# Router shift on VectorE, expert-stage ends by halves, the norm's scale on a diagonal, fillers at the last load

## What is computed

```
h  = rms_norm(x, norm1_g) * (1 + scale1) + shift1
x  = x + gate1 * mixer(h)
h  = rms_norm(x, norm2_g) * (1 + scale2) + shift2
x  = x + gate2 * hier_moe(h)
```

## Time and profile before

| | |
|---|---|
| median of 3 runs | 1050.4 us (1048.04 to 1050.93) |
| the profiled execution's own time | 1042.98 us |
| span of its trace | 1041.2 us |
| mean granted TensorE clock | 0.949 of full speed |
| PE busy | 905.2 us, 87% of the span |
| DVE, ACT, POOL busy | 314.3, 197.3, 34.2 us |
| moved by DMA | 329.18 MB, mean 316 GB/s |
| chain that ended last | PE 70%, DMA 19%, DVE 3%, SP's queue 3%, ACT 2% |

### The profile page before, as it was taken

How to read it: one execution, slowest core, us unless ns; L and a number is a source line. 1 busy time by engine, 2 the same in 40 slices (tenths; PEclk the granted TensorE clock), 3 DMA queues, 4 the chain that set the end, 5 groups by cost and what they waited for, 6 DMA issues and landing times.

```text
span 1041.2 us, 14206 instructions
## 1 busy us (share of the span) xinstructions
PE 905.2 (87%) x5967; PEld 516.2 (50%) x5967; DVE 314.3 (30%) x774; ACT 197.3 (19%) x366; POOL 34.2 (3%) x62
## 2 busy tenths in 40 slices
PE   1799999979699787997699999999996997789963
PEld 0586556664565444564244444444445654455531
DVE  1120235831732111110277814231037221111203
ACT  3111112340211100100340013543002111111102
POOL 3000000111000000000000000001000000000000
PEclk9899999999799999998889999999997998899987
DMA  9999746999597999999943555146835979999995
GB/s 313 401 389 373 284 172 235 409 414 401 191 408 275 421 421 420 421 421 416 394 174 127 191 193 217 41 162 255 348 137 211 377 299 420 422 420 419 421 416 218
DMA packets 74088, 329.18 MB, mean 316 GB/s; under 512 B 5773, under 2 KB 6149, under 8 KB 50213
## 3 DMA queue, kind: packets, MB, share of 16 engines
q1 hardware_dynamic: 69012, 313.44, 76.0%
q0 software_dynamic: 4400, 13.35, 3.5%
q10 hardware_dynamic: 608, 1.44, 0.4%
HBM read 322.11 MB, written 6.09 MB: 315 GB/s over the span
## 4 chain that ended last, share of the span: by engine, by line
PE 70%; DMA 19%; DVE 3%; SPq 3%; ACT 2%; issue 1%; DVEq 0%
PE PS L763 68%; DMA ring<-in_moe_w_gate 11%; DMA ring<-in_mod_w 5%; DMA ring<-in_moe_w_down 4%; SPq L635 1%; SPq L642 1%; SPq L648 1%; ACT scratch L1421 0%; ACT HT L1428 0%; DVE H L1819 0%; DVE X L1814 0%; PE PS L796 0%; DVE scratch L2013 0%; PE PS L1363 0%; PE PS L1093 0%
## 5 line engine op out<-in xcount | busy, mean ns | idle before, releaser
L763 PE MATMUL PS<-ring,scratch 128*32 128x256 f32 (+3 forms) x2592 | 294.5, 461 | 58.8 <-DMA ring<-in_moe_w_gate 39.7
L763 PEld LDWEIGHTS PS<-ring,scratch 128*32 128x32 f32 (+2 forms) x2592 | 140.2, 127 | 205.8 <-issue 158.1
L763 PE MATMUL PS<-ring,HT 128*128 128x512 f32 x432 | 191.9, 598 | 2.7 <-ACT HT L1428 1.9
L763 PEld LDWEIGHTS PS<-ring,HT 128*128 128x128 f32 x432 | 81.2, 191 | 99.2 <-issue 95.5
L763 PE MATMUL PS<-scratch 128*128 128x512 f32 (+3 forms) x480 | 115.9, 427 | 4.6 <-DVE scratch L2477 2.9
L763 PE MATMUL PS<-scratch,H 128*128 128x128 f32 x640 | 84.2, 288 | 3.1 <-DVE scratch L2183 3.1
L763 PEld LDWEIGHTS PS<-scratch 128*128 128x128 f32 (+2 forms) x480 | 56.0, 184 | 59.3 <-issue 51.2
L763 PEld LDWEIGHTS PS<-scratch,H 128*128 128x128 f32 x640 | 79.1, 202 | 10.5 <-issue 10.5
L2296 DVE TENSOR_TENSOR scratch<-PS,scratch 128x256 f32<-128x256 f32 x20 | 8.5, 424 | 188.2 <-ACT scratch L1610 188.2
L763 PE MATMUL PS<-ring,cpad 128*32 128x256 f32 x768 | 48.2, 401 | 18.7 <-DMA ring<-in_mod_w 18.7
L763 PE MATMUL PS<-ring,modrows 128*128 128x512 f32 x120 | 52.5, 592 | 0.0
(11 more groups left out here) (307 smaller groups left out, 707.0 us busy)
## 6 DMA issues: line engine op xcount, KB each, us to landing
ring<-in_moe_w_up SPq DMA_DIRECT2D x64, 1024.0 KB, 18.6
ring<-in_moe_w_gate SPq DMA_DIRECT2D x56, 1024.0 KB, 16.8
ring<-in_moe_w_down SPq DMA_DIRECT2D x56, 1024.0 KB, 16.9
ring<-in_mod_w SPq DMA_DIRECT2D x24, 2048.0 KB, 16.7
ring<-in_odd_w_in SPq DMA_DIRECT2D x12, 2048.0 KB, 12.9
ring<-in_even_w_in SPq DMA_DIRECT2D x7, 2048.0 KB, 16.2
ring<-in_moe_w_down SPq DMA_DIRECT2D x16, 512.0 KB, 17.7
ring<-in_odd_w_out SPq DMA_DIRECT2D x4, 2048.0 KB, 7.6
```

The lines of the kernel that those rows point to most:

```text
L763: return nc.tensor.matmul(out, lhsT, rhs, start=start, stop=stop, skip_group_check=True, **kw)
```

## The change

- *logit_shift*: DVE (*router_shift*) multiplies the router weights by the shift column and sums the eight tiles into LSHIFT for both streams; PE then sums over partitions with one product with ones, for both streams at once, and adds the bias with another. For layer 0 it stands between the two chunks of *project_out*, for layer 1 in the second last step alone.
- *project_out*: PE's turns of stream 1 by halves are placed ahead of stream 0's logits by halves.
- *scale_h(1)* and *shift_h(1)* become *gain_h(1)* (X * GAIN, in *mixer_end*) and *finish_h(1)* (times rstd plus SHIFT, after the mask). *order* is moved ahead of the first *compare* and *build*, its second copy (*keep_rank*) stays behind them.
- Ends of expert stages: one semaphore step per stream and half; the last scatter waits for each half of YG by itself; *moe_end* multiplies by halves, and adds stream 1 by halves; ACT squares stream 1 by halves (*mean_square_halves*). *inverse_std* of the last norm moves to the output loop.
- Six products of the identity with itself are placed on PE behind the first half of the last step's down weights.
- *xhat* goes; DVE writes DIAG = identity * rstd (*diagonal*), and PE turns X by a product with it (*turn_norm*), both in layer 0 and layer 1.

The diff, cut:

```diff
-SHIFT_AT = (NSTEP - 3, NSTEP - 2)
+SHIFT_AT = NSTEP - 2
...
+        DIAG = normed[:, :, 0:P]
...
-            pool.wait_ge(router_ready, 3)
+            pool.wait_ge(router_ready, 2)
             router_weights(1)
...
+            def logit_shift(l, bank):
                 pe.wait_ge(late_params_in, 16 * 12)
+                pe.wait_ge(lshift_ready, l + 1)
+                at = PS[:, bank, 0:128].rearrange("p (s n) -> p s n", s=S)[:, :, 0:NG + NE]
+                matmul(at, cst("ones"), LSHIFT[:, :, :], True, False)
+                matmul(at, cst("ones")[0:1, :], bcast(rbias[:, l:l + 1, :], [1, S, NG + NE]), False, True)\
+                    .then_inc(lshift_done, 1)
+            def turn_norm(s):
                 for k in range(KT):
-                    matmul(at, bcast(COLS[:, l, COL_OF[3], s, k:k + 1], [P, P]), RW[:, k, :], k == 0, False)
+                    mm = matmul(PS[:, 2 * s + k // 4, P * (k % 4):P * (k % 4) + P], X[:, s, P * k:P * k + P], DIAG[:, s, :],
+                                True, True)
+                mm.then_inc(ht_done, 1)
...
+                    if l == 0 and q == 0:
+                        logit_shift(0, 5)
                 pe.wait_ge(x_ready, 2 * n + 1)
                 turn_stream(0, X)
-                pe.wait_ge(router_ready, 3 * (l + 1))
                 for half in range(2):
+                    if half:
+                        pe.wait_ge(x_ready, 2 * n + 2)
+                    else:
+                        pe.wait_ge(x_half, 2 * l + 1)
+                    for k in range(4 * half, 4 * half + 4):
+                        mm = nc.tensor.transpose(PS[:, 2 + half, P * (k % 4):P * (k % 4) + P],
+                                                 X[:, 1, P * k:P * k + P], ident)
+                    mm.then_inc(ht_done if half else ht_half, 1)
+                    if not half:
+                        pe.wait_ge(router_ready, 2 * (l + 1))
                     pe.wait_ge(xt_ready_a, 4 * l + half + 1)
                     logits(l, 0, [half])
...
-            for s in range(S):
-                logit_shift(0, s, 5)
             pe.wait_ge(mix_ready, 4)
             project_out("even_out", 2, HT, 0)
...
+                            if not j:
+                                for _ in range(6):
+                                    matmul(PS[:, 6, 0:P], ident, ident, True, True)
...
                 for s in range(S):
-                    scatter((NSTEP - 1) % 2, streams=[s]).then_inc(moe_done, 1)
+                    for half in range(2):
+                        if not s and half:
+                            pe.wait_ge(yg1_ready, NSTEP * (l + 1))
+                        matmul(PS[:, 2 * s + half, :], WSELT[:, (NSTEP - 1) % 2, s, :], YG[:, half, :], False, False)\
+                            .then_inc(moe_done, 1)
...
+            def mean_square_halves(n, junk):
+                act.wait_ge(x_half, n)
+                square(junk[:, 0:BANK], X[:, 1, 0:BANK], sumsq[:, 1:2])
+                act.wait_ge(sq_ready, squared[0])
+                A_(first_half_mean, sumsq[:, 1:2], IDENTITY, scale=1.0 / D, bias=EPS_COL)
+                act.wait_ge(x_ready, 2 * n)
+                square(junk[:, BANK:], X[:, 1, BANK:], second_half_sum)
+                root(second_half_sum, first_half_mean, 1)
...
-                def xhat(s):
-                    act.wait_ge(rstd_ready, 2 * n + s + 1)
-                    A_(normed[:, s, :], X[:, s, :], IDENTITY, scale=rstd[:, s:s + 1]).then_inc(xhat_ready, 1)
...
+            def router_shift(l):
+                dve.wait_ge(router_in, 32 * (l + 1))
+                dve.wait_ge(cols_ready, 4 * l + 4)
+                for s in range(S):
+                    st.mark(V.tensor_tensor(RWG[:, s, :, :], RW[:, :, :],
+                                            bcast(COLS[:, l, COL_OF[3], s, :].unsqueeze(2), [P, KT, NG + NE]), ALU.mult))
+                st.wait()
+                for s in range(S):
+                    ins = V.tensor_reduce(LSHIFT[:, s, :], RWG[:, s, :, :].rearrange("p k n -> p n k"), AX, ALU.add)
...
+            def diagonal(n, s):
+                dve.wait_ge(rstd_ready, 2 * n + s + 1)
+                V.tensor_scalar(DIAG[:, s, :], ident, rstd[:, s:s + 1], None, ALU.mult).then_inc(diag_ready, 1)
...
+            def gain_h(n, s):
+                dve.wait_ge(x_half, n + 1)
+                dve.wait_ge(x_ready, 2 * n + s + 1)
+                st.mark(V.tensor_tensor(H[:, s, :, :].rearrange("t k p -> t p k"),
+                                        X[:, s, :].rearrange("t (p k) -> t p k", k=KT),
+                                        GAIN[:, s, :].rearrange("t (p k) -> t p k", k=KT), ALU.mult))
...
                 shift_h(0)
+                gain_h(n, 1)
                 inverse_std(n + 1, 1)
...
             def moe_end(n):
+                l = n // 2
                 dve.wait_ge(gate_in, 32 * (n + 1))
+                for s in range(S):
+                    g = last_gate(l, s)
+                    for half in range(2):
+                        cols = slice(BANK * half, BANK * half + BANK)
+                        dve.wait_ge(moe_done, 4 * l + 2 * s + half + 1)
+                        st.mark(V.tensor_tensor(g[:, cols], PS[:, 2 * s + half, :], g[:, cols], ALU.mult))
+                    st.wait()
+                    if not s:
+                        V.tensor_tensor(X[:, 0, :], X[:, 0, :], g, ALU.add).then_inc(x_ready, 1)
+                        continue
+                    if not l:
+                        inverse_std(n + 1, 0)
+                        diagonal(n + 1, 0)
+                    for half in range(2):
+                        cols = slice(BANK * half, BANK * half + BANK)
+                        V.tensor_tensor(X[:, 1, cols], X[:, 1, cols], g[:, cols], ALU.add)\
+                            .then_inc(x_ready if half else x_half, 1)
+                if not l:
+                    inverse_std(n + 1, 1)
+                    diagonal(n + 1, 1)
...
-                scale_h(2 * l + 1, 1)
+                finish_h(2 * l + 1, 1)
...
+                order()
                 for s in range(S):
                     st.mark(compare(PLACE[:, 0, :], s, (0,))[0])
                 st.wait()
                 for s in range(S):
                     build(PLACE[:, 0, :], s, 0).then_inc(sel_ready, 1)
-                order()
-                shift_h(1)
+                keep_rank()
```

More of the change, by code:

```diff
@@ L1154, in step @@
                         scatter(1 - par, i == 1)
-                    if l == 0 and i in SHIFT_AT:
-                        logit_shift(1, SHIFT_AT.index(i), 4)
+                    if l == 0 and i == SHIFT_AT:
+                        logit_shift(1, 4)
                     late = late_state(l, i)
@@ L1166, in step @@
                     gate_or_up(1, sl[1], par).then_inc(used, len(sl[1]))
-                    if l == 0 and i in SHIFT_AT:
-                        pe.wait_ge(router_ready, 5 + SHIFT_AT.index(i))
+                    if l == 0 and i == SHIFT_AT:
+                        pe.wait_ge(router_ready, 4)
                     if not last:
@@ L1413, in load_sqrt, with square, root @@
                 A_(small[:, 153 + n:154 + n], EPS_COL, SQRT)
+            squared = [0]
+            def square(junk, x, total):
+                squared[0] += 1
+                A_(junk, x, SQUARE, accum_out=total).then_inc(sq_ready, 1)
+            def root(total, bias, s):
+                act.wait_ge(sq_ready, squared[0])
+                A_(sumsq[:, s:s + 1], total, SQRT, scale=1.0 / D, bias=bias).then_inc(std_ready, 1)
             def mean_square(n, s, junk):
@@ L1737, in _ @@
             load_sqrt(4)
-            for s in range(S):
-                mean_square(4, s, squares[:, s, :])
+            mean_square(4, 0, squares[:, 0, :])
+            mean_square_halves(4, squares[:, 1, :])
             act.wait_ge(y_ready, 3)
@@ L1826, in shift_h, with finish_h @@
                 V.tensor_tensor(h, h, SHIFT[:, s, :].rearrange("t (p k) -> t p k", k=KT), ALU.add).then_inc(h_ready, 1)
+            def gain_h(n, s):
[4 more added lines that the diff above has]
+                                        GAIN[:, s, :].rearrange("t (p k) -> t p k", k=KT), ALU.mult))
+            def finish_h(n, s):
+                dve.wait_ge(rstd_ready, 2 * n + s + 1)
+                h = H[:, s, :, :].rearrange("t k p -> t p k")
+                V.scalar_tensor_tensor(out=h, in0=h, scalar=rstd[:, s:s + 1],
+                                       in1=SHIFT[:, s, :].rearrange("t (p k) -> t p k", k=KT),
+                                       op0=ALU.mult, op1=ALU.add).then_inc(h_ready, 1)
             def mixer_end(n, item):
@@ L1831, in mixer_end @@
                 dve.wait_ge(first_out, n // 2 + 1)
-                residual(n, 0)
+                residual(0, GATE[:, 0, :])
                 inverse_std(n + 1, 0)
@@ L1879, in _ @@
                 inverse_std(0, s)
+                diagonal(0, s)
             dve.wait_ge(bias_in, 16 * 12)
@@ L2063, in _ @@
```

(9 more changed lines are left out.)

80 lines of the change are left out of this document (32 added, 48 removed).

## The result

The changed kernel took 1033.8 us (median of 4 runs, 1031.55 to 1035.72) beside 1049.2 us of the kernel before (4 runs, 1045.35 to 1050.93): ratio 0.986, 95% interval 0.982 to 0.989.

The account below looks back on a forecast made before the run. TensorE starts each expert stage, then weight loads set its rate; gains lie ahead of and behind it. Terms -0.6 -1.2 -4.4 -3.0 +0.4 = -8.8 on the 1050.4 us median gave 1041.6 us, range 1036 to 1047.2 (8 in 10).

Parts of the forecast that it names:

- the base: Differences came from the profiled execution (1042.98 us) and were set against the median (1050.4), as if the 7.4 us stayed.
- Part 4: End of the first expert stage: held clock, earlier scatter and changed turns win 3.0 us, between 2 and 5.
- Part 1: Router shift on VectorE, first layer: output product ends 3.0 us earlier, but the SHIFT wait leaves 0.6 us won.
- part 2: Reordered router in both layers: logits read and gathers start earlier, 0.6 us per layer, 1.2 in all.
- Part 3: End of the last stage: fillers and work by halves win 4.4 us; last store at A+11.6, A being the last weights' landing.
- Part 5: Start: the two turns by products take about 1.8 us more, partly hidden; 0.4 us lost, between 0 and 2.
- The fillers don't hold the clock: Rival (0.15): waits behind the last loads still end at the lower clock; 4.4 us less gain, 1046.0 us.
- SHIFT rows in time: Rival (0.14): in the first layer the SHIFT rows land before they are wanted; 3.0 us won there, 1039.2 us.
- A turn is four transposes' time: Rival (0.06): a turn by products takes 4.4 us instead of 2.05, at start and first stage's end; 1046.9 us.
- The loads set the early expert steps too: Rival (0.08): what earlier gathers win is given back in the expert stages, 1.8 us lost; 1043.4 us.
- Slower through the SHIFT rows: Rival (0.03): SHIFT rows land late and hold up VectorE's scaling and the router; landing at 272 means +3.5, 1053.9 us.

Follow-up runs that it names:

- after: The changed kernel as first measured, with its first trace: profiled execution 1035.72 us, median 1033.8 us, ratio 0.986 to the kernel before.
- after_again: The changed kernel run once more without any edit, with a second trace: 1033.1 us, ratio 0.986 to the kernel before.
- own_sem: The changed kernel with a separate semaphore for the SHIFT rows, awaited only by the addition that reads them: 1029.7 us, ratio 0.985 to the kernel before.
- before_again: The kernel before, unchanged, run once more for its times and a second trace: 1046.5 us, ratio 1.000.
- router_fill_more: The changed kernel with a separate SHIFT semaphore and 19, 7 and 6 filler products in TensorE's router waits: 1026.9 us, ratio 0.980 to the kernel before.
- router_fill: The changed kernel with a separate SHIFT semaphore and 14, 4 and 5 filler products in TensorE's router waits: 1030.6 us, ratio 0.983 to the kernel before.
- own_sem_again: The changed kernel with a separate semaphore for the SHIFT rows, run a second time: 1029.2 us, ratio 0.984 to the kernel before.
- start_back: The changed kernel with the old norm (scaled copy, transposes) at the start only: 1034.9 us, ratio 0.990 to the kernel before.

## Why the prediction was wrong

Sign and mechanisms were mostly right; the number was 7.8 us too high, half from the base and half from terms. The steps that failed are the base, the router of layer 0 behind the SHIFT wait, the landing of the last store, and what follows the first odd product's start in part 4.

**The base.** "I take the differences from the profiled execution and set them against the median, as if those 7.4 us stayed." Three runs were too few: the 57 later ones have medians of 1045.6 to 1046.9. Some 4 us of the 7.8 are this. The spread I allowed (2.9 us) was that of the same three; it is 9.6. 1046.3 less the 12.9 of the account would have been 1033.4.

**Part 1 and layer 0's share of part 2** (-1.2): nothing. Counted from the last attention pass, the output product ended 2.8 us earlier (3.0 forecast). The trap was named, "*scale_h(0)* on DVE, which waits for all four rows of GAIN and SHIFT", and its price for stream 1 was about right: its residual began 0.4 us earlier in after and 1.4 in after_again, where 0.6 was forecast. What failed is the step behind it, PE's "4 turns and 24 passes of 0.12, some 3.6 us", with the logits "set by DVE and no longer by PE". The pause of PE that the trap makes (2.96 and 1.98 us), and the half clock behind it, were not in the sum: the 24 passes took 5.2 us in both traces, 2.77 in own_sem, and DVE waited 3.40 and 2.46 us for them. That took back the 2.8 us. own_sem shows the price: 3.6 us in that stretch. The Trainium skill, "DMA: Bandwidth & Descriptors" (section Queues, rings and completion order), had each DMA engine take turns between queues with work, so that the earlier load could only slow the rows. The traces agree in the sign, with little between them: the last SHIFT row of layer 0 took 24.9 to 25.9 us in the ten traces with the new order, 22.7 to 25.0 in the three with the old.

**Part 2 in layer 1** (-0.6): 0.3 at the gathers, 1.2 more behind them. The logits were read 4.2 us behind x_ready, with DVE last, as forecast. Between 226.0 and 227.4 us that stage varies with the clock at its gathers too, so how much of the 1.2 is the earlier sorted order stays open.

**Part 3** (-4.4): 4.5 to the last issue (A+11.5, A+11.6 forecast). Missed: the 1.1 behind it. I priced the issue and took the landing behind it as unchanged.

**Part 4** (-3.0): 4.5. To the first odd product it won 2.8 (520.02 less 506.86 in after_again, 524.17 less 508.20 in before_again), where the steps gave 3.4. Behind it 1.7 more were won, and there stands the failed step, the second turn and what follows, "another 0.4 to 1.2, as the pauses ahead of it probably still drop the clock": the clock was back, the second turn took 1.95, and the first odd product 1.98 where it had been 3.75. The size of that depends on where the half clock falls: the kernels with fillers and diagonal won 3.5 to 5.2 in this stretch, all above the 3.0.

**Part 5** (+0.4): no loss that the traces show, for the longer turn lies in a wait for a load that was longer (2.66) in the typical trace than the 1.41 I had read.

**Rivals.** "The fillers don't hold the clock" fell: without them 3.7 to 4.8 us are lost. "SHIFT rows in time" fell with part 1. "A turn is four transposes' time" fell: 1.95 for eight tiles, 1.09 by transposes at the same clock. The Trainium skill, "TensorE: Matmul & The Clock Gate" (section Terms), has the transpose mode four times faster for FP32; here the ratio is 1.8. "The loads set the early expert steps too" fell in router_fill_more. "Slower through the SHIFT rows" named the right place, but stream 1 was as late as before (262.83 and 262.43), not 9 us later.

## What to carry to other kernels

A short wait that nothing hides can have two prices: itself, and the lower clock for the work behind it; fill it with products nobody reads for as long as it lasts, and look at the clock during the fillers too, for those of router_fill ran at half clock themselves. Give each load that is read at a different point its own semaphore: a shared one makes the first reader wait for the last load. And take the base of a forecast from as many executions as show the spread: a profile from one end of the spread and three runs from the other cost as much here as all mis-sized terms.

## What was not expected of the hardware

The granted clock fell or stayed up behind the same pause of 2.5 us in two executions (3.50 and 1.92 for the same 16 passes). At the odd layer's first turn it fell in after_again and own_sem_again (3.49 and 3.53 for 16 passes) and stayed up in own_sem, start_back and router_fill_more (2.05), behind the same pause of 2.42 us. In the router it fell with idle times of 4.6, 1.4 and 1.65 us and stayed up when no more than 0.65 of each was left; with 1.42 and 0.99 left in layer 0, and 1.76 and 0.99 in layer 1, it fell all the same. And of the 3.2 us between two traces of before, 3.0 arose ahead of 260 us; whether that holds for the spread of all runs, no trace shows.
